# A hybrid attention and state-space block: the state-space stage with its features on partitions, its decay rows spread by transfers, and a softmax with its sink apart

## The reference, cut to what matters

```python
u = rmsnorm(h, mix_pre_norm)
q, k, v, z, xbc, dt_raw, g_a, g_b = split(u @ w_in)
# attention: 16 query heads, 4 key/value heads, window of 2 chunks of 64, a learned sink per head
probs = softmax(concat([scores, sink], -1))[..., :-1]
# state space: 4 groups of 8 heads, head width 64, state 128
x, B, C = split(silu(causal_dwconv(xbc)))
dt = softplus(dt_raw + dt_bias);  a_cs = cumsum(dt * a)
y  = ((C B^T) * exp(a_cs[l] - a_cs[s]) masked) @ (x * dt)   # within a block: "diagonal" part
y += exp(a_cs) * (C @ state)                                # from the state before the block
y += x * d_skip
y  = rmsnorm_per_group(y * silu(z)) * norm_w                # group = 512 features
merged = sigmoid(g_a) * (attn @ w_attn_out) + sigmoid(g_b) * (y @ w_ssd_out)
```

## Time and profile before

| | |
|---|---|
| median of 3 runs | 1079.98 us (1079.81 to 1080.94) |
| profiled execution, its own time | 1081.87 us |
| its span | 1079.8 us |
| TensorE busy | 1059.3 us, 98% |
| VectorE busy | 645.3 us, 60% |
| ScalarE busy | 454.7 us, 42% |
| GpSimd busy | 124.6 us, 12% |
| transfers' share of 16 DMA engines | 28.7% |
| granted TensorE clock | full in all 40 slices (2.4 GHz) |

### The profile page before, as it was taken

How to read it: one execution, slowest core, us unless ns; L and a number is a source line. 1 busy time by engine, 2 the same in 40 slices (tenths; PEclk the granted TensorE clock), 3 DMA queues, 4 the chain that set the end, 5 groups by cost and what they waited for, 6 DMA issues and landing times.

```text
span 1079.8 us, 13848 instructions
## 1 busy us (share of the span) xinstructions
PE 1059.3 (98%) x5353; PEld 888.5 (82%) x5353; DVE 645.3 (60%) x867; ACT 454.7 (42%) x714; POOL 124.6 (12%) x196
## 2 busy tenths in 40 slices
PE   8999999999999999999999999999999999999997
PEld 8888888878888887788888888788888888888886
DVE  4897777776777777842433233466666666651214
ACT  4664456445654565532321213363434344431112
POOL 6013300330033013200000003120000000000001
PEclk9999999999999999999999999999999999999999
DMA  6321132114202420232233243413424233323211
GB/s 189 118 69 30 40 117 69 30 40 123 81 13 58 138 79 1 79 100 95 78 117 99 96 162 129 137 41 78 116 78 115 80 110 84 110 92 110 82 74 78
DMA packets 108426, 95.39 MB, mean 88 GB/s; under 512 B 12175, under 2 KB 98523, under 8 KB 108379
## 3 DMA queue, kind: packets, MB, share of 16 engines
q1 hardware_dynamic: 108379, 94.74, 28.7%
HBM read 92.63 MB, written 2.10 MB: 88 GB/s over the span
## 4 chain that ended last, share of the span: by engine, by line
PE 85%; DVE 8%; ACT 3%; POOL 2%; issue 1%; DMA 1%; POOLq 0%; DVEq 0%; SPq 0%; ACTq 0%
PE ps L1200 18%; PE ps L1201 18%; PE ps L1202 18%; PE ps L1207 8%; PE ps L1208 8%; PE ps L1209 8%; PE ps L1486 2%; DVE wlo L793 1%; ACT whi L449 1%; DVE conv L902 1%; PE ps L1427 1%; PE ps L1239 1%; POOL xdtd L403 1%; PE ps L1498 1%; PE ps L1478 1%
## 5 line engine op out<-in xcount | busy, mean ns | idle before, releaser
L793 DVE TENSOR_TENSOR wlo<-raw,whi 128x2048 fp32r<-128x2048 f32 (+2 forms) x83 | 188.5, 2272 | 209.8 <-ACT whi L449 209.8
L1200 PE MATMUL ps<-uhi,whi 128*128 128x512 f32 x640 | 249.6, 390 | 0.1
L1202 PE MATMUL ps<-uhi,wlo 128*128 128x512 f32 x640 | 249.1, 389 | 0.0
L1201 PE MATMUL ps<-ulo,whi 128*128 128x512 f32 x640 | 249.0, 389 | 0.0
L449 ACT ACTIVATE whi<-raw 128x2048 fp32r<-128x2048 f32 (+2 forms) x83 | 155.2, 1871 | 175.5 <-PE ps L1209 93.0
L1200 PEld LDWEIGHTS ps<-uhi,whi 128*128 128x128 f32 x640 | 120.2, 188 | 25.1 <-DVE zg L1011 0.2
L1202 PEld LDWEIGHTS ps<-uhi,wlo 128*128 128x128 f32 x640 | 120.1, 188 | 24.9
L1201 PEld LDWEIGHTS ps<-ulo,whi 128*128 128x128 f32 x640 | 120.2, 188 | 24.6
L1207 PE MATMUL ps<-whi,uhi 128*128 128x512 f32 (+2 forms) x304 | 115.3, 379 | 2.0 <-DVE wlo L793 1.8
L1209 PE MATMUL ps<-wlo,uhi 128*128 128x512 f32 (+2 forms) x304 | 112.6, 370 | 0.0
L1208 PE MATMUL ps<-whi,ulo 128*128 128x512 f32 (+2 forms) x304 | 112.6, 370 | 0.0
(11 more groups left out here) (230 smaller groups left out, 1466.9 us busy)
## 6 DMA issues: line engine op xcount, KB each, us to landing
raw<-in_w_in_dram SPq DMA_DIRECT2D x24, 1024.0 KB
raw<-in_w_up_dram SPq DMA_DIRECT2D x44, 512.0 KB
raw<-in_w_down_dram SPq DMA_DIRECT2D x11, 1024.0 KB
raw<-in_w_in_dram SPq DMA_DIRECT2D x16, 512.0 KB
raw<-in_w_ssd_out_dram SPq DMA_DIRECT2D x8, 1024.0 KB
raw<-in_w_attn_out_dram SPq DMA_DIRECT2D x4, 1024.0 KB
raw<-in_w_out_dram SPq DMA_DIRECT2D x4, 1024.0 KB
yT<-in_x_dram SPq DMA_DIRECT2D x4, 512.0 KB, 4.9
```

What stands on the lines that cost most here:

```text
L793: dve.tensor_tensor(wlo[sl][:, 0:width] if into is None else into, raw[sl][:, 0:width], h.bitcast(F32), ALU.subtract).then_inc(s["lo_done" ...
L1200: pe.matmul(bank(b)[:, span], hi_[:, k, c], ah[:, span], start=first and k == 0, stop=False)
L1201: pe.matmul(bank(b)[:, span], hi_[:, k, c], al[:, span], start=False, stop=False)
L1202: ins = pe.matmul(bank(b)[:, span], lo_[:, k, c], ah[:, span], start=False, stop=last and k == KD - 1)
```

## The change

- **Decays.** `sums`, `build`, `seg_hi`, `seg_lo` and `above` are gone. Once, in group 0, a small product gives the running sums of dt times a with (tile, head) on partitions; ScalarE stores them and their exponentials, and SP writes both to a scratch in DRAM. In each step SP spreads 8 rows of sums over all 128 partitions (`spread_sums`, 4 KB to each partition, 512 KB), and in steps 1 to 3 the 8 rows of exponentials (`spread_growth`, as large). ScalarE forms each head's differences with a Relu and a per-partition bias, four heads at a time, and then exponentiates (`gains`).
- **Output turned round.** y is formed with features on partitions (`products`): the 64 columns of one head are the weights and the 128 columns of `decay_m` (or of `c_dec`) stream through, even heads writing partitions 0 to 63 and odd heads 64 to 127. C times the state is scaled beforehand: GpSimd multiplies C by the spread exponentials (`c_dec`, 128 x 1024), so one product of 512 columns becomes eight of 128. `turn_y` is gone.
- **z** is also formed with features on partitions, one tile of 24 matmuls at a time: two tiles in step 0, one each in steps 1 and 2, none in step 3.
- **Step 3** of a group is spread over the next group's first block (q, k, v), or over `gate_a` after the last group. The blocks of weights that were split in step 3 and at the group's end are split in steps 2 and 3.
- **Norm.** Gating, squaring, summing and scaling are done once for each group: four products, four squares, three sums, four small matmuls with ones (`norm_sums`), a mean, a root, a store of 128 x 4 roots to DRAM and a load of them spread to all partitions (`spread_roots`), and four products (`normalize`).
- **Skip.** x times d_skip is a scaled copy on ScalarE (`skip_x`, four for each group) in place of GpSimd's `xd`.
- **Softmax.** The sink has its own 4 columns: one more 4-column exponential on ScalarE and one more 4-column addition on VectorE; the sum and the exponential work on 512 columns, not 516.

```diff
+            def spread_sums(g, t):
+                sp.wait_ge(s["fell"], 2 * (g * NT + t))
+                sp.dma_start(sums_bc[:, :, :].rearrange("p h l -> p (h l)"), sums_of(g, t)[0].partition_broadcast(P)).then_inc(s["sums_in"], 16)
+            def spread_growth(g, t):
+                sp.wait_ge(s["grown"], g * (NT - 1) + t - 1)
+                sp.dma_start(grow_bc[:, :, :].rearrange("p h l -> p (h l)"), sums_of(g, t)[1].partition_broadcast(P)).then_inc(s["grow_in"], 16)
+            def spread_roots(g):
+                sp.wait_ge(s["root_ok"], g + 1)
+                sp.dma_start(root_scr[g], small[:, 20:24]).then_inc(s["roots_out"], 16)
+                sp.wait_ge(s["roots_out"], 16 * (g + 1))
+                sp.dma_start(conv[:, 3, :], root_scr[g].rearrange("p t -> (p t)").partition_broadcast(P)).then_inc(s["roots_in"], 16)
...
+                        sp.wait_ge(s["rows_ok"], 2)
+                        sp.dma_start(sum_scr.rearrange("a r l -> r a l"), sum_rows).then_inc(s["rows_out"], 16)
+                        sp.wait_ge(s["rows_out"], 16)
+                        spread_sums(0, 0)
+                spread_growth(g, 1)
+                if g < NG - 1:
+                    qkv_half(g + 1, 0)
+                else:
+                    put(N_C1, [(wide(0), rows_of(w_in, 0, KD, C_GA, 256))])
+                spread_sums(g, 1)
...
+                for t in range(2, NT):
+                    spread_sums(g, t)
+                    spread_growth(g, t)
...
+            for i in range(1, NG):
                 put(N_C1 + 2 * i, [(wide(0), rows_of(w_in, 0, KD, C_GA + 256 * i, 256))])
                 put(N_C1 + 2 * i + 1, [(wide(1), rows_of(w_at, 0, KD, 256 * i, 256))])
+                if i == 1:
+                    spread_roots(NG - 1)
...
+            def root_y(G):
+                pool.wait_ge(s["mean_ok"], G + 1)
+                pool.wait_ge(s["roots_out"], 16 * G)
+                link(pool.tensor_scalar(small[:, 20:24], small[:, 16:20], 4 * EPS, None, ALU.add))
+                pool.tensor_tensor(small[:, 20:24], small[:, 20:24], small[:, 0:1].to_broadcast([P, NT]), ALU.pow).then_inc(s["root_ok"], 1)
...
+                    pool.wait_ge(s["grow_in"], 16 * (G * (NT - 1) + t + 1))
+                    pool.wait_ge(s["silu_ok"], G * 6 + 2)
+                    pool.wait_ge(s["y_mm"], T + 1 if t else T)
+                    pool.tensor_tensor(c_dec[:, :, :], grow_bc[:, :, :],
+                                       conv[:, 1, (t + 1) * P:(t + 2) * P].unsqueeze(1).to_broadcast([P, SH, P]),
+                                       ALU.mult).then_inc(s["grown"], 1)
...
+            def mean_y(G):
+                act.wait_ge(s["norm_mm"], G + 1)
+                act.wait_ge(s["root_ok"], G)
+                act.activation(small[:, 16:20], ps[:, 7, 0:NT], ACT.Copy, scale=1.0 / XW).then_inc(s["mean_ok"], 1)
...
+            def square_y(G):
+                for f in range(4):
+                    act.wait_ge(s["gated"], G * 4 + f + 1)
+                    act.activation(conv[:, 2 + f, :], yT[:, G * 4 + f, :], ACT.Square).then_inc(s["squared"], 1)
...
+                def gains(t, half):
+                    T = G * NT + t
+                    if half == 0:
+                        act.wait_ge(s["sums_in"], 16 * (T + 1))
+                        act.wait_ge(s["decay_ok"], 1)
+                        act.wait_ge(s["y_mm"], T)
+                    for h in range(4 * half, 4 * half + 4):
+                        at = G * SH + h
+                        ins = act.activation(decay_m[:, h, :], sums_bc[:, h, :], ACT.Relu, scale=-1.0, bias=sum_s[:, t, at:at + 1])
+                    ins.then_inc(s["fell"], 1)
+                    if half:
+                        for q in range(2):
+                            act.wait_ge(s["fell"], 2 * T + q + 1)
+                            m = decay_m[:, 4 * q:4 * q + 4, :]
+                            act.activation(m, m, ACT.Exp, scale=-1.0).then_inc(s["lexp"], 1)
...
+                def skip_x(f):
...
+                    act.activation(conv[:, 2 + f, :], conv[:, 2 + f, :], ACT.Copy,
+                                   scale=skip[:, G * 4 + f:G * 4 + f + 1]).then_inc(s["skip_ok"], 1)
...
                     act.wait_ge(s["pT_mm"], T + 1)
                     act.activation(pT[:, :, :].rearrange("p h l -> p (h l)"), bank(4), ACT.Copy).then_inc(s["pT_sb"], 1)
+                    if t < NT - 1:
+                        gains(t + 1, 0)
                     act.wait_ge(s["o_mm"], T + 1)
                     act.activation(oT[:, bass.ds(G * 2, 2), t * P:(t + 1) * P],
...
+                    if t < NT - 1:
+                        gains(t + 1, 1)
...
+            def gate_y(G):
+                dve.wait_ge(s["zg_ok"], G * 4 + 4)
...
+                for f in range(4):
+                    y = yT[:, G * 4 + f, :]
+                    dve.tensor_tensor(y, y, zg[:, f, :], ALU.mult).then_inc(s["gated"], 1)
...
+            def sum_squares(G):
+                dve.wait_ge(s["squared"], G * 4 + 4)
+                for a, b in ((2, 3), (4, 5), (2, 4)):
+                    ins = dve.tensor_tensor(conv[:, a, :], conv[:, a, :], conv[:, b, :], ALU.add)
...
+            def normalize(G):
+                dve.wait_ge(s["roots_in"], 16 * (G + 1))
...
+                    y = yT[:, G * 4 + f, :]
+                    y = y.rearrange("p (t c) -> p t c", t=NT)
+                    dve.tensor_tensor(y, y, roots, ALU.mult).then_inc(s["yn_ok"], 1)
...
+                    def maximum():
+                        dve.wait_ge(s["s_mm"], T + 1)
...
+                        dve.wait_ge(s["pT_mm"], T)
+                        dve.tensor_tensor(probs[:, :, :].rearrange("p (a b) k -> p a b k", a=2), sc,
+                                          mx.unsqueeze(3).to_broadcast([P, 2, 2, P]), ALU.subtract)
+                        dve.tensor_tensor(sm[:, 3, :].rearrange("p (a b) -> p a b", a=2), sinkg, mx, ALU.subtract).then_inc(s["smx"], 1)
+                    def divide():
+                        dve.wait_ge(s["sexp"], T + 1)
+                        link(dve.tensor_reduce(sm[:, 0, :], probs[:, :, :], AX_X, ALU.add))
+                        link(dve.tensor_tensor(sm[:, 2, :], sm[:, 0, :], sm[:, 3, :], ALU.add))
+                        link(dve.reciprocal(sm[:, 3, :], sm[:, 2, :]))
+                        dve.tensor_tensor(probs[:, :, :], probs[:, :, :], heads(sm[:, 3, :], QH, P), ALU.mult).then_inc(s["p_ok"], 1)
...
+                    masked_cb()
...
                     else:
+                        maximum()
+                        masked_gains()
                         times_dt()
...
+                        divide()
+                    if t < NT - 1:
+                        gate(t + 1)
+                    if t == 2:
+                        lo_next(6, 4 * QKV if G < NG - 1 else BLK)
                     if t == NT - 1:
-                        lo_next(6, 4 * QKV if G < NG - 1 else BLK)
...
+                    dve.wait_ge(s["skip_ok"], G * 4 + 4)
+                    dve.tensor_tensor(yT[:, G * 4:G * 4 + 4, c], bank(2 + t % 2).rearrange("p (f c) -> p f c", f=4), conv[:, 2:6, c],
+                                      ALU.add).then_inc(s["y_done"], 1)
...
+            def products(G, t, weights, moving, first, last):
+                for h in range(SH):
+                    r = slice((h % 2) * HD, (h % 2 + 1) * HD)
+                    ins = pe.matmul(ps[r, 2 + t % 2, (h // 2) * P:(h // 2 + 1) * P], weights[:, h * HD:(h + 1) * HD],
+                                    moving[:, h, :], start=first if t == 0 else first and h < 2, stop=last if t == 0 else last and h >= SH - 2)
+                return ins
+            def diagonal(G, t):
+                T = G * NT + t
...
+                products(G, t, xdt, decay_m, t == 0, True).then_inc(s["y_mm"], 1)
...
+            def norm_sums(G):
...
+                pe.wait_ge(s["sq_ok"], G + 1)
+                pe.wait_ge(s["st_ok"], (G + 1) * (NT - 1))
+                for t in range(NT):
+                    ins = pe.matmul(ps[:, 7, t:t + 1], conv[:, 2, t * P:(t + 1) * P], ones[:, 0:1], start=True, stop=True)
+                ins.then_inc(s["norm_mm"], 1)
...
+                        if h == 0 and t == 0:
+                            diagonal(G - 1, NT - 1)
+                        elif h == 0 and t == 1:
+                            turn_p(G - 1, NT - 1)
+                        elif h == 0 and t == 2:
+                            weigh_values(G - 1, NT - 1)
+                if G:
+                    norm_sums(G - 1)
...
+                    if t < NT - 1:
+                        z_tile(t + 1)
+                        turn_p(G, t)
                     if t:
                         pe.wait_ge(s["st_ok"], G * (NT - 1) + t)
-                        pe.matmul(bank(6), conv[:, 1, c], state[:, :], start=True, stop=True)
...
+                        pe.wait_ge(s["grown"], G * (NT - 1) + t)
+                        if T > 1:
```

(15 more changed lines are left out.)

564 lines of the change are left out of this document (248 added, 316 removed).

## The result

The changed kernel takes 1069.3 us (median of 4 runs, 1068.5 to 1069.7), the kernel before 1080.5 beside it (1079.8 to 1082.8): a ratio of 0.9892 (95% interval 0.9875 to 0.9909), 11.2 us less. The forecast was 17 less. Direction and range held; a third of the gain did not come. The profiled execution's span is 1066.8 us, against 1079.8.

A forecast was written before the change was run, and what follows sets the result against it. TensorE, busy 98% of the span, was taken as the bound. Savings of 20.0 us for four groups, plus 0.4 and 1.2, less 4.7, gave 17 off the 1080.0 median: 1063 us, own range 1052 to 1070, with two rivals 1052 to 1082.

The forecast's parts named there:

- Work taken and added: TensorE's work in each group: 15.4 us taken, 8.6 added, so 6.8 less (1.2 to 8.3).
- the 0.95 in front of it: Each `products` call on TensorE: 0.95 us with halves partly side by side, plus 0.15 for entering the shape, 1.1 in all.
- the first rival: In `products`, halves do not run side by side with 128 columns: 1.9 us a call, 1082 us in all; chance 0.12.
- the fourth: In `products`, each record waits for its weight load: 4.2 us a call, 1150 us in all; chance 0.02.
- Waits in the steps: New TensorE waits in a group's steps, for `probs`, ScalarE's copy of v's product and step 3: 1.8 us a group.
- has twelve more z matmuls ahead of its transposes and opens no wait: Step 0 of each group: with more z matmuls as cover, TensorE was to have no new wait.
- The diagonal part's wait in step 3: TensorE's wait for masks and `xdt` before step 3's diagonal part stays: about 1.1 us, as against 0.6.
- The second rival: `c_dec` on GpSimd slows VectorE, so steps 1 and 2 stay at 12.8 us: 1074 us in all; chance 0.17.
- After the last group: The roots' round trip, not hidden behind `gate_a`: TensorE waits 4.0 us, plus some 0.7 before, 4.7 once.
- The 0.7 of an earlier wait: After the last group, squares and sums delay the first `lo`, costing TensorE some 0.7 us ahead of the 4.0 wait.
- Transfers: Spreads of sums and growth for the next step: 7.1 us together within 8.4, hidden with 1.3 us to spare.
- a clock below full: Sign for the profile after, with no place or size given: a granted clock below full would upset the whole forecast.

The follow-up runs named there:

- halves_in_row: The changed kernel with the eight heads of `products` taken as 0, 2, 4, 6, 1, 3, 5, 7, not in turn; 1078.1 us, ratio 0.9965 to the kernel before.
- cdec_later: The changed kernel with GpSimd's first `c_dec` of a group waiting for step 0's diagonal part; 1064.1 us, ratio 0.9837 to the kernel before.
- decay_first: The changed kernel with the state's multiplication by its decay moved ahead of y's addition in steps 1 and 2; 1066.9 us, ratio 0.9868 to the kernel before.
- roots_later: The changed kernel with the last group's four scalings by the roots moved behind the second `gate_a` on VectorE; 1059.8 us, ratio 0.9799 to the kernel before.

## Why the prediction was right, and where it was short

**Work taken and added.** Busy time of TensorE a period: 103.7 before, 97.3 after, 6.3 less, forecast 6.8. By starts the calls are cheaper than forecast: 3 x 1.03 and 2 x 1.90, 6.9 a group, for 7.4 (7 x 1.1, less 2 x 0.15). The entry of 0.15, paid once by two calls side by side, was right; mis-sized was the 0.95 in front of it, which is 0.88, half of 1.76. The page "TensorEngine Tiling (Array Packing)" of the Trainium skill, section "Theoretical Speedup", gives up to twofold: 0.88 was its value, and the rows agree (1.03 less 0.15, against 1.76). halves_in_row shows the cause, and the first rival (1.9 a call) fell with it. So did the fourth, exposed weight loads, 4.2 a call.

**Waits in the steps.** Forecast 1.8 us more a group, measured about 2.4 more: for `probs` 1.05, 0.27 and 0.79, for the state 0.49, for `xdt` 0.3 and three times 0.38 for the copy of v's product, 4.0, against 1.6 before (0.6 and 0.6, and 0.43 once). Steps 1 and 2 were 11.67 and 12.18 long, forecast 11.9. The step that failed is the sentence that step 0 "has twelve more z matmuls ahead of its transposes and opens no wait". It looked at TensorE's cover only, and not at what GpSimd does at that moment: the first `c_dec` of a group waits only for the diagonal part of the step before, the last of the previous group, and so starts right behind `xdtd`, beside the division. The prediction had put every `c_dec` at the end of a diagonal part. The diagonal part's wait in step 3 was taken too long (1.1; it is 0.3 and 0.5 for the state before it). The errors in work and waits, 0.5 and 0.6 of opposite sign, nearly cancel: 5.24 a group for 5.3, which is luck in part.

**The second rival was half true.** It named the right mechanism, `c_dec` slowing VectorE, with the two durations of `xdtd` in the earlier trace rows as its sign; it took it for all or nothing, with a chance of 0.17. It is in the changed kernel in 12 of 12 places, at 1.3 us in eight and 2.2 in four, most of which the steps hide; cdec_later and decay_first bring back 5.9 and 2.6 of it. The trace of before had the rule, if one asks what VectorE did at the two rows of `xdtd` in the earlier trace rows, 1.04 us at 217.91 and 2.43 at 230.40. VectorE's timeline of before:

```profile
217.68 0.68 DVE L1011 SCALAR_TENSOR_TENSOR zg<-tanh_z,ps 128x512 f32<-128x512 f32 x1
...
230.17 1.75 DVE L793 TENSOR_TENSOR wlo<-raw,whi 128x1536 fp32r<-128x1536 f32 x1
```

Beside the gate, which reads PSUM (`ps`), `xdtd` is quick. Beside the weight remainder, with both operands in SBUF and 0.23 us ahead, it ends 1 us after the remainder does: it waited and then ran. The prediction saw "a busy VectorE" and not which instruction. "SBUF — State Buffer" of the Trainium skill, section "Who interferes with whom", states just that: a VectorE instruction with two inputs in SBUF contends with a GpSimd instruction that reads SBUF, and issue order decides who blocks. The traces here agree, in both directions (VectorE 2.38 for 0.16, GpSimd 2.40 for 1.05), and for the PSUM operand too (0.69, begun 0.6 behind `c_dec`, in decay_first).

**After the last group.** This is the term that was mis-sized: 4.7 forecast, 8.8 measured, by roots_later 9.5 of span. In the round trip: mean and root 1.6 (forecast 1.3), store 1.4 and spread 5.4 (2.0 and 4), four scalings 4.0 (2.7), splits 2.7 (2.8), `lo` 2.3 (2.3): 17.4 for 15.1, less a cover of 11.0 (forecast 11.1). The 0.7 of an earlier wait did not come. Some 0.8 from the transfers, 1.3 from scalings whose second operand is read at a step of four elements (1.06 to 1.11 us each, where the gating of the same size takes 0.68; the step as cause was not tested alone). And 2.5 from the clock, which the prediction left out: it said that a clock below full would upset it, but did not ask whether its own longest wait would bring that about.

**Transfers.** Hidden, as forecast. The spread of the sums landed 4.5 us after its issue (median of 16), that of the growth 5.7; the pair was through about 3 us before it was read, with 1.3 us forecast.

**From the span to the runs.** The profiled executions differ by 13.0, the medians by 11.2. The profiled execution of before took 1.4 more than the median of 1080.5, that of after 0.4 less than its own. In the first the first 32 records of x's transposes took 5.6 us, in the second 3.8. The traced executions of the other kernels have either 3.8 or 5.3 to 5.7, so this is no part of the change. What it is stays open: from 8 to 10 us TensorE has 11 of these records before and 20 after, and the profile gives the clock as full in both. It is as large as the difference (1.8); the prediction had taken its 17 from the median although the profiled execution was above it. So of the 5.8 us between 17 and 11.2, 4.1 are the term after the last group and some 0.7 TensorE's wait there for ScalarE's copy of `probs` (0.69), which no longer has the diagonal part to cover it; about 1 is left that no term names.

## What to carry to other kernels

When a change puts a larger instruction on GpSimd, lay its time beside VectorE's: in these traces every VectorE instruction with both operands in SBUF that started within it lasted until about its end or beyond, and the profile shows this as the duration of the waiting instruction, not as idle time. Put such an instruction where VectorE reads PSUM or idles, and let the one that is on the critical path start first. And when a round trip through memory stands in an engine's queue, look at what is queued behind it: here one line moved two places down gave back nearly as much as the whole change.

## What the runs showed of the hardware that was not expected

- A four-column VectorE addition took 2.38 us beside GpSimd's product and 0.16 without.
- Whoever starts second waits: the same state multiplication took 0.69 when 0.13 us ahead of `c_dec`, 2.85 when 0.5 us behind.
- After 6.4 us of waiting TensorE started 12 matmuls 0.43 us apart, and then 0.23 again; with the wait filled with matmuls they were 0.23 apart from the second on.
- Eight products with 64 columns of weights, standing alone, took 1.03 us with the halves alternating, 1.51 with four of a half in a row; alternating, their records started in pairs.
